# Expert stage of a four-layer fp32 model: three groups gathered at once, three passes written out, one looped

## The chip, the cores and the metric

The kernel runs on one core of a Trainium2 chip. The metric is the device time of one launch in microseconds (us), the median of several runs.

## The reference

Two blocks of two layers each, over 256 tokens of width 1024, all in fp32. Each layer has a mixer and then a hierarchical mixture of experts. This is the part that the change touches; layers 0 and 1 have 4 groups of 4 experts and also add a gated term, layers 2 and 3 have 4 groups of 8 experts.

```python
def hier_moe(h, wgc, bgc, wgf, bgf, w1, w3, w2):
    ...
    pg = jax.nn.softmax(jnp.dot(t, wgc, preferred_element_type=f32) + bgc.astype(f32), axis=-1)
    gw, gi = lax.top_k(pg, 1)
    fl = (jnp.dot(t, wgf, preferred_element_type=f32) + bgf.astype(f32)).reshape(T, N_GROUPS, EXPERTS_PER_GROUP)
    ...
    tv, ti = lax.top_k(jax.nn.softmax(fs, axis=-1), TOP_K_IN_GROUP)
    ...
    a = jnp.einsum('td,edf->tef', t, w1)
    c = jnp.einsum('td,edf->tef', t, w3)
    act = jax.nn.silu(a) * c * gates[:, :, None].astype(t.dtype)
    y = jnp.einsum('tef,efd->td', act, w2)

# first block, layers 0 and 1:
        y_ple = jax.nn.sigmoid(h @ ple_wg[i] + ple_bg[i]) * (p[i] @ ple_wp[i])
        h = layer_norm(DN_ALPHA * h + y_moe + y_ple, ln2_g[i], ln2_b[i])
```

Each token picks one group and two experts in it. A group has its own expert weights; a group that more than 128 tokens picked needs a second pass over the same weights.

## The kernel before

**The stream of weights.** All large weights come as units of 1 MB (128 x 2048 fp32). Four queues run in a fixed order over the same units: SyncE starts two DMAs of 512 KB into one of `RING` = 4 slots (`load`, L388 to L394) as soon as the unit four places earlier has been split; ScalarE copies the unit to a rounded high part (`split`, L1298 to L1304), for which one of `PARTS` = 3 buffers must be free, so the unit three places earlier used up; VectorE subtracts it for the low part (`split`, L1776 to L1781); TensorE multiplies high by high, low by high and high by low (`three`, L622 to L625), always 128 x 512 wide here. So one unit is 12 matmuls where one block of 128 tokens is used and 24 where both are.

**One expert** is three units: two for the two input projections (`up(e, 0)`, `up(e, 1)`, 24 matmuls) and one for the output projection (`down(e)`, 12 matmuls). Between them ScalarE makes the silu (L1386), VectorE multiplies it with the other half and the gate (L2040), TensorE transposes the product (L783), ScalarE and VectorE make its high and low parts (L1394, L2049), and `down(e)` follows. The order on TensorE is `up(e, 0)`, transposes of expert e - 1, `up(e, 1)`, `down(e - 1)`, so that this chain is covered by the next expert's matmuls.

**One pass** handles up to 128 tokens of one group: E experts (4 in layers 0 and 1, 8 in layers 2 and 3). All passes are iterations of one hardware loop on each engine (`Fori(0, passes)`, L761 on TensorE, L1373, L2025), 4 of them with these inputs (the program allows 5). The tokens of a pass are gathered by matmuls with a 0/1 matrix `SP` (32 matmuls of 128 x 128 in two parts, `gather`, L735 and L736, and four for the gates, L741, L742). The first part of the next gather and the gates are put around the transposes of the last expert, ahead of `down(E - 1)`; the second part comes at the head of the next iteration. The result of pass p - 1 is scattered in pass p, after `up(0, 1)`, by 8 matmuls of 128 x 512 (`scatter`, L750), in the first pass with zeros. After the loop comes the last scatter, and VectorE adds the four banks to X (L2070).

**Ahead of the loop** (`experts`, L676, L1321, L1886): transposes of the tokens (L640), logits (48 matmuls with the tokens stationary and 20 or 36 columns moving), some 55 small VectorE instructions that wait for each other and choose the group, the two experts, the gates (up to L1944), the slot `KEY` of each token (up to L1956) and the table of passes (up to L1968); then all engines read the number of passes, TensorE clears six banks (L727), VectorE builds `SP` (L2006), and the first gather follows. In layers 0 and 1 four units of 24 matmuls (the gated term) lie between; GpSimd multiplies and adds that term (L588 to L592). In layer 1 the 16 transposes of the second block's memory input lie there as well.

## Time and profile before

| | |
|---|---|
| median of 3 runs | 1811.83 us (1811.3 to 1812.22) |
| the profiled execution | 1805.22 us, of which the profile spans 1803.4 us |
| mean granted TensorE clock | 0.936 |
| TensorE matmul busy | 90% of the span |
| VectorE, ScalarE, GpSimd busy | 73%, 58%, 7% |
| DMA | 402.36 MB, mean 223 GB/s |

The profile lists for each group of instructions the line, the engine, the operation with the tiles that it writes and reads, a count, the busy time and the mean duration of one. In a timeline each row has the start and the duration in us, and in brackets how long the engine had stood idle and what ended that. Matmuls overlap, so a row's duration is longer than the distance to the next; distances between starts are used here. The busy share of TensorE is modelled in the same way and is an upper bound.

### The profile page before, as it was taken

To read this page: it belongs to the slowest core of one execution; us is meant where nothing else is said; L and a number is where in the kernel's file an instruction comes from. 1 tells how busy PE (TensorE), PEld (TensorE's weight loads), DVE (VectorE), ACT (ScalarE), POOL (GpSimd) and SP (SyncE) were. 2 spreads that over 40 slices of the span, in tenths; PEclk is the share of its full clock that TensorE was granted. 3 is DMA by queue.
4 is the path that set the end of the run, shared out by engine and by line. 5 is a ranking of instruction groups with operands and counts; after the bars stand their busy time and mean duration, and the time that the engine had idled before them with its cause. 6 is when DMAs were issued, how large, how long until landed. Compare 5 with 4: busy or idle time off the path is not lost.

```text
span 1803.4 us, 22655 instructions
## 1 busy us (share of the span) xinstructions
PE 1616.8 (90%) x7718; PEld 1332.0 (74%) x7718; DVE 1314.4 (73%) x1614; ACT 1038.5 (58%) x1151; POOL 129.1 (7%) x195
## 2 busy tenths in 40 slices
PE   5997999969879799979978999999798869999997
PEld 4876777858767678858866887878687657878786
DVE  6757588876667688874656878888775458888886
ACT  3543477744434577636424777777475326777774
POOL 3001400030022300000010000000000200000000
PEclk9997899989998899999977999999899959999998
DMA  8324388865334588844424989999542309999995
GB/s 309 125 92 154 116 296 304 301 226 171 128 96 155 179 306 306 307 168 141 152 86 158 364 294 342 335 306 369 162 144 71 97 24 302 312 362 306 361 313 186
DMA packets 282833, 402.36 MB, mean 223 GB/s; under 512 B 15962, under 2 KB 220538, under 8 KB 282512
## 3 DMA queue, kind: packets, MB, share of 16 engines
q1 hardware_dynamic: 273632, 381.99, 62.1%
q0 software_dynamic: 9136, 19.54, 3.7%
q8 instruction: 36, 0.59, 0.1%
q14 instruction: 29, 0.24, 0.0%
HBM read 400.43 MB, written 1.05 MB: 223 GB/s over the span
## 4 chain that ended last, share of the span: by engine, by line
PE 55%; DVE 19%; ACT 9%; DMA 9%; issue 7%; SPq 1%; DVEq 0%; ACTq 0%
PE bank L623 15%; PE bank L625 14%; PE bank L624 14%; DVE w_lo_at L1779 8%; ACT w_hi_at L1303 6%; DMA raw_at<-in_moe_w_up_dram 4%; PE bank L640 2%; DMA raw_at<-in_moe_w_down_dram 2%; DMA raw_at<-in_w_in_dram 1%; PE bank L735 1%; PE bank L736 1%; DMA raw_at<-in_moe_w_dram 1%; PE bank L830 1%; DVE x_at L1834 1%; DVE sel_at L2006 1%
## 5 line engine op out<-in xcount | busy, mean ns | idle before, releaser
L1779 DVE TENSOR_TENSOR w_lo_at<-raw_at,w_hi_at 128x2048 fp32r<-128x2048 f32 (+1 forms) x365 | 830.7, 2283 | 179.1 <-ACT w_hi_at L1303 168.6
L1303 ACT ACTIVATE w_hi_at<-raw_at 128x2048 fp32r<-128x2048 f32 (+1 forms) x365 | 694.1, 1907 | 102.9 <-PE bank L625 48.6
L623 PE MATMUL bank<-w_hi_at,xs_hi_at 128*128 128x512 f32 x768 | 315.2, 410 | 9.1 <-DVE w_lo_at L1779 5.5
L625 PE MATMUL bank<-w_hi_at,xs_lo_at 128*128 128x512 f32 x768 | 304.1, 396 | 0.0
L624 PE MATMUL bank<-w_lo_at,xs_hi_at 128*128 128x512 f32 x768 | 302.8, 394 | 0.0
L623 PE MATMUL bank<-w_hi_at,t_hi_at 128*128 128x512 f32 (+3 forms) x560 | 223.8, 400 | 17.2 <-DVE t_lo_at L1786 5.2
L624 PE MATMUL bank<-w_lo_at,t_hi_at 128*128 128x512 f32 (+3 forms) x560 | 216.9, 387 | 0.0
L625 PE MATMUL bank<-w_hi_at,t_lo_at 128*128 128x512 f32 (+3 forms) x560 | 216.8, 387 | 0.0
L623 PEld LDWEIGHTS bank<-w_hi_at,xs_hi_at 128*128 128x128 f32 x768 | 146.4, 191 | 50.0 <-DVE w_lo_at L1779 13.1
L625 PEld LDWEIGHTS bank<-w_hi_at,xs_lo_at 128*128 128x128 f32 x768 | 145.9, 190 | 33.3
L624 PEld LDWEIGHTS bank<-w_lo_at,xs_hi_at 128*128 128x128 f32 x768 | 146.4, 191 | 27.9
L623 PE MATMUL bank<-w_hi_at,act_hi_at 128*128 128x512 f32 x384 | 154.4, 402 | 9.6 <-DVE act_lo_at L2049 9.4
L624 PE MATMUL bank<-w_lo_at,act_hi_at 128*128 128x512 f32 x384 | 152.4, 397 | 0.0
L625 PE MATMUL bank<-w_hi_at,act_lo_at 128*128 128x512 f32 x384 | 152.0, 396 | 0.0
L623 PEld LDWEIGHTS bank<-w_hi_at,t_hi_at 128*128 128x128 f32 x560 | 109.0, 195 | 42.6 <-issue 17.7
L625 PEld LDWEIGHTS bank<-w_hi_at,t_lo_at 128*128 128x128 f32 x560 | 108.6, 194 | 20.6
L624 PEld LDWEIGHTS bank<-w_lo_at,t_hi_at 128*128 128x128 f32 x560 | 109.1, 195 | 18.9 <-issue 0.5
L1394 ACT ACTIVATE act_hi_at<-bank 128x256 fp32r<-128x256 f32 x96 | 36.8, 383 | 112.4 <-PE bank L783 73.3
L623 PEld LDWEIGHTS bank<-w_hi_at,act_hi_at 128*128 128x128 f32 x384 | 72.5, 189 | 30.5 <-issue 13.3
L625 PEld LDWEIGHTS bank<-w_hi_at,act_lo_at 128*128 128x128 f32 x384 | 72.9, 190 | 17.4
L624 PEld LDWEIGHTS bank<-w_lo_at,act_hi_at 128*128 128x128 f32 x384 | 72.8, 190 | 15.5
L1386 ACT ACTIVATE silu_at<-bank 128x256 f32<-128x256 f32 x96 | 36.8, 384 | 78.2 <-PE bank L625 77.6
(485 smaller groups left out, 2089.3 us busy)
## 6 DMA issues: line engine op xcount, KB each, us to landing
raw_at<-in_moe_w_dram SPq DMA_DIRECT2D x192, 512.0 KB, 4.9
raw_at<-in_moe_w_gate_dram SPq DMA_DIRECT2D x128, 512.0 KB, 5.0
raw_at<-in_moe_w_up_dram SPq DMA_DIRECT2D x128, 512.0 KB, 6.0
raw_at<-in_moe_w_down_dram SPq DMA_DIRECT2D x128, 512.0 KB, 5.4
raw_at<-in_w_in_dram SPq DMA_DIRECT2D x40, 512.0 KB, 5.2
raw_at<-in_a_w_in_dram SPq DMA_DIRECT2D x20, 512.0 KB, 4.7
raw_at<-in_w_out_dram SPq DMA_DIRECT2D x16, 512.0 KB, 4.3
raw_at<-in_ple_wg_dram SPq DMA_DIRECT2D x16, 512.0 KB, 4.9
```

What stands on the lines that cost most here:

```text
L623: pe.matmul(out, ah, bh, start=start, stop=False, skip_group_check=loose)
L624: pe.matmul(out, ah, bl, start=False, stop=False, skip_group_check=loose)
L625: return pe.matmul(out, al, bh, start=False, stop=stop, skip_group_check=loose)
L640: ins = pe.transpose(BK[b][:, c * T + tb * P:c * T + tb * P + P], block_, IDENT)
L735: pe.matmul(o, HH[:, tb, a:a + P], SP[:, tb, :], start=tb == 0, stop=False)
L736: ins = pe.matmul(o, HL[:, tb, a:a + P], SP[:, tb, :], start=False, stop=tb == 1)
L830: ins = pe.matmul(out, mat[:, kb, cols], rhs(kb), start=kb == 0, stop=kb == 1)
L1303: act.activation(WH[:, s.part(), 0:width], RAW[:, s.slot(), 0:width], ACT.Copy).then_inc(hi_done, 1)
L1386: act.activation(SIL[:, :], BK[6 + e % 2][:, 0:256], ACT.Silu).then_inc(*m.silu.tick(e))
L1394: act.activation(AH[:, :, :], BK[6 + e % 2][:, 0:256].rearrange("p (c t) -> p c t", t=P), ACT.Copy).then_inc(*m.ah.tick(e))
L1779: dve.tensor_tensor(WL[:, s.part(), 0:width], RAW[:, s.slot(), 0:width], WH[:, s.part(), 0:width].bitcast(F32), ALU.subtract).then_inc(spl ...
L1834: go(dve.scalar_tensor_tensor(x_, x_, by[:, tb:tb + 1], ROW[:, slot, 0:width], op1, op2))
```

## The change

- **Passes.** The first three passes (groups 0, 1, 2) are written out and chained: `up(0, 0)` of pass p + 1 follows `down(E - 2)` of pass p, with the transposes of the last expert behind it and `down(E - 1)` behind `up(0, 1)`. The loads follow the same order and the first three groups' need no table. Only the passes from the fourth on (one, with these inputs) run in a hardware loop, with their own gather; the loop body begins with the first half of the gather, the last expert's transposes and `down(E - 1)` of the pass before.
- **Gather.** The three groups' tokens are gathered at once: 8 chunks of four matmuls of 128 x 384 (`SP3`), each chunk in a bank of its own, copied out as `XH3` and `XL3`. They go ahead of the computing of the gates, and the matmuls that gather the gates go behind the first expert's `up`.
- **Logits.** The router's weights are stationary (high and low part side by side, `RWHL`), the 256 tokens move: 16 matmuls, one ScalarE copy with the bias, four fp32 matmuls that turn the result (`turn_logits`).
- The clearing of banks is gone (the first scatter starts them), and so is the first pass's scatter of zeros. The routing's slot arithmetic is shorter. The scatter comes behind `up(1, 0)`.
- GpSimd's work on the gated term moves to VectorE (`gated`), in two halves.
- The memory input's transposes move from layer 1's prelude into its third pass, one group per expert.
- Two splits of expert units are put ahead of the last `add_and_measure` steps in layers 2 and 3.

```diff
             def experts(L):
...
-                for tb in range(TB):
-                    for c in range(DC):
-                        t_ = slice(tb * P, tb * P + P)
-                        ins = three(BK[6][:, tb * 64:tb * 64 + NR[L]], TH[:, c, t_], TL[:, c, t_],
-                                    RWH[:, c, 0:NR[L]], RWL[:, c, 0:NR[L]], c == 0, c == DC - 1)
+                for c in range(DC):
+                    pe.matmul(BK[6][0:2 * N, 0:T], RWHL[:, c, 0:2 * N], TH[:, c, :], start=c == 0, stop=False,
+                              skip_group_check=True)
+                    ins = pe.matmul(BK[6][0:N, 0:T], RWHL[:, c, 0:N], TL[:, c, :], start=False, stop=c == DC - 1,
+                                    skip_group_check=True)
...
-                for b in range(6):
-                    ins = pe.matmul(BK[b][:, :], ZR[:, :], HH[:, 0, 0:512], start=True, stop=True)
-                ins.then_inc(*small_ready.tick(("cleared", L)))
...
+                pe.wait_ge(*dve_ready.at(("sel", L)))
+                for c, b in enumerate(GATHER):
+                    claim(b)
+                    o, a = BK[b][:, 0:3 * P], slice(c * P, c * P + P)
+                    for tb in range(TB):
+                        pe.matmul(o, HH[:, tb, a], SP3[:, tb, :], start=tb == 0, stop=False)
+                        ins = pe.matmul(o, HL[:, tb, a], SP3[:, tb, :], start=False, stop=tb == 1)
+                    ins.then_inc(*gathered.tick((L, c)))
+                    owner[b] = xl_ready.at((L, c))
...
+                for p in range(3):
+                    cols = slice(p * P, p * P + P)
+                    for e in range(E):
...
+                        before = (p, e - 1) if e else (p - 1, E - 1)
+                        if (p, e) == (0, 0):
+                            pe.wait_ge(*xl_ready.at((L, 3)))
+                        claim(6 + e % 2)
+                        up(e, 0, (XH3, XL3), cols)
+                        if e == 1 and p:
+                            claim(2, 3)
+                            scatter(p - 1, p == 1)
+                        if (p, e) == (0, 0):
+                            pe.wait_ge(*xl_ready.at((L, 7)))
+                        else:
+                            turn_glu(*before)
+                        up(e, 1, (XH3, XL3), cols)
+                        if (p, e) == (0, 0):
+                            key_row()
+                            gates()
+                        else:
+                            claim(4, 5)
+                            down(*before, memory)
...
+                with pe.Fori(3, passes) as p:
...
+                    pe.wait_ge(*m.sel.at(p - 3))
+                    gather(0).then_inc(*m.gather_a.tick())
+                    turn_glu(p - 1, E - 1, gather_gates)
+                    down(p - 1, E - 1)
+                    gather(1).then_inc(*m.gather_b.tick())
+                    pe.wait_ge(*m.xl_a.at(p - 3))
+                    up(0, 0, (XH, XL))
+                    pe.wait_ge(*m.xl_b.at(p - 3))
+                    up(0, 1, (XH, XL))
+                    for e in range(1, E):
+                        up(e, 0, (XH, XL))
+                        if e == 1:
+                            scatter(p - 1)
+                        turn_glu(p, e - 1)
+                        up(e, 1, (XH, XL))
+                        down(p, e - 1)
```

VectorE's order in a written-out step and at the head of the loop body:

```diff
+                            glu(*before, gate3(*before))
+                            split()
+                            if e == 1:
+                                slots(ch)
+                                low_y(p - 1)
+                            split()
+                            low(*before)
...
+                with dve.Fori(3, passes) as p:
...
+                    glu(p - 1, E - 1, GS[:, E - 1:E])
+                    split()
+                    low_x(0, m.xh_a, m.xl_a, p)
+                    split()
+                    dve.wait_ge(*m.at.at(p - 1, E - 1))
+                    dve.tensor_copy(GS[:, :], BK[7][:, 256:264]).then_inc(*m.gs.tick())
+                    low(p - 1, E - 1)
+                    low_x(1, m.xh_b, m.xl_b, p)
+                    slots(lc)
+                    low_y(p - 1)
```

## Rows read from the trace of the kernel before

**Rows 1.** Windows: stretch, length, busy time by engine, granted clock, DMA share, GB/s.
```profile
934.00:966.00 32.00, 19.85 (x85) 18.60 (x84) 14.45 (x63) 5.64 (x7) 0.00 (x0) 0.50 0.10 34
1122.00:1198.00 76.00, 75.23 (x353) 61.38 (x353) 64.30 (x51) 55.02 (x46) 0.00 (x0) 1.00 0.99 333
```
**Rows 2.** Timeline of ScalarE, layer 2, third pass: the same step, one expert apart.
```profile
1159.53 1.91 ACT L1303 ACTIVATE w_hi_at<-raw_at 128x2048 fp32r<-128x2048 f32 x1
...
1168.07 1.91 ACT L1303 ACTIVATE w_hi_at<-raw_at 128x2048 fp32r<-128x2048 f32 x1
```
**Rows 3.** Timeline of TensorE, layer 2, between second and third pass, and at the end.
```profile
1111.58 0.44 PE L623 MATMUL bank<-w_hi_at,act_hi_at 128*128 128x512 f32 x1
...
1114.40 0.22 PE L735 MATMUL bank<-sel_at,tok_hi_at 128*128 128x128 f32 x1
...
1117.65 0.47 PE L623 MATMUL bank<-w_hi_at,act_hi_at 128*128 128x512 f32 x1 [0.71 <-DVE act_lo_at L2049]
...
1127.97 0.39 PE L750 MATMUL bank<-ys_hi_at,sel_t_at 128*128 128x512 f32 x1
...
1129.79 0.39 PE L623 MATMUL bank<-w_hi_at,xs_hi_at 128*128 128x512 f32 x1
...
1263.15 0.40 PE L623 MATMUL bank<-w_hi_at,act_hi_at 128*128 128x512 f32 x1
```
**Rows 4.** The page, costliest groups: the two splits.
```profile
L1779 DVE TENSOR_TENSOR w_lo_at<-raw_at,w_hi_at 128x2048 fp32r<-128x2048 f32 (+1 forms) x365 | 830.7, 2283 | 179.1 <-ACT w_hi_at L1303 168.6
L1303 ACT ACTIVATE w_hi_at<-raw_at 128x2048 fp32r<-128x2048 f32 (+1 forms) x365 | 694.1, 1907 | 102.9 <-PE bank L625 48.6
```
**Rows 5.** Timeline of ScalarE, layer 2, second pass: three units apart.
```profile
1095.48 1.92 ACT L1303 ACTIVATE w_hi_at<-raw_at 128x2048 fp32r<-128x2048 f32 x1 [0.70 <-DMA raw_at<-in_moe_w_up_dram]
...
1104.20 1.92 ACT L1303 ACTIVATE w_hi_at<-raw_at 128x2048 fp32r<-128x2048 f32 x1 [0.70 <-DMA raw_at<-in_moe_w_up_dram]
```
**Rows 6.** Timeline of VectorE: the adds that end each layer's expert stage.
```profile
384.50 2.48 DVE L2070 TENSOR_TENSOR x_at<-x_at,bank 128x512 f32<-128x512 f32 x4 [2.23 <-PE bank L750]
...
774.21 2.48 DVE L2070 TENSOR_TENSOR x_at<-x_at,bank 128x512 f32<-128x512 f32 x4 [2.27 <-PE bank L750]
...
1276.70 2.48 DVE L2070 TENSOR_TENSOR x_at<-x_at,bank 128x512 f32<-128x512 f32 x4 [2.77 <-PE bank L750]
...
1796.37 2.48 DVE L2070 TENSOR_TENSOR x_at<-x_at,bank 128x512 f32<-128x512 f32 x4 [3.15 <-PE bank L750]
```
**Rows 7.** Timeline of VectorE, layer 2, end of the second pass.
```profile
1113.60 0.47 DVE L2040 SCALAR_TENSOR_TENSOR glu_at<-silu_at,gate_sel_at,bank 128x256 f32<-128x256 f32 x1
```
**Rows 8.** Timeline of layer 2 ahead of its loop, TensorE and VectorE.
```profile
931.83 0.26 PE L623 MATMUL bank<-rw_hi_at,t_hi_at 128*128 128x36 f32 x1 [1.50 <-DVE t_lo_at L1786]
...
940.27 0.30 DVE L1908 TENSOR_TENSOR logits_at<-bank,route_b_at 128x36 f32<-128x36 f32 x2 [5.18 <-PE bank L625]
...
949.47 0.16 DVE L1956 TENSOR_TENSOR key_at<-v_at,v_at 128x2 f32<-128x2 f32 x1
...
955.43 0.48 DVE L2006 TENSOR_SCALAR sel_at<-consts_at,key_at 128x128 fp32r<-128x128 f32 x2 [0.84 <-DVE key_row_at L1998]
...
966.37 0.73 PE L623 MATMUL bank<-w_hi_at,xs_hi_at 128*128 128x512 f32 x1
```
**Rows 9.** Timeline of layer 0 ahead of its loop, TensorE, GpSimd and VectorE.
```profile
200.69 0.39 PE L625 MATMUL bank<-w_hi_at,t_lo_at 128*128 128x512 f32 x1
...
204.03 2.40 POOL L588 TENSOR_TENSOR y_at<-y_at,sg_at 128x1024 f32<-128x1024 f32 x1
...
204.20 3.53 DVE L2006 TENSOR_SCALAR sel_at<-consts_at,key_at 128x128 fp32r<-128x128 f32 x2 [1.10 <-issue]
...
214.10 0.73 PE L623 MATMUL bank<-w_hi_at,xs_hi_at 128*128 128x512 f32 x1
```
**Rows 10.** Timeline of TensorE: first expert matmul of layers 1 and 3.
```profile
600.22 0.45 PE L623 MATMUL bank<-w_hi_at,xs_hi_at 128*128 128x512 f32 x1
...
1486.55 0.73 PE L623 MATMUL bank<-w_hi_at,xs_hi_at 128*128 128x512 f32 x1
```

More of the change, by code:

```diff
@@ L477, in _ @@
+                s.unit, s.turns = unit, sp.snap(start + (passes - 3) * turns)
+                last = sp.value_load(TAB[0:1, bass.ds(passes, 1)], min_val=0, max_val=3)
+                down(last, E - 1)
             for tb in range(TB):
@@ L819, in experts @@
+                s.unit, s.turns = unit, pe.snap(start + (passes - 3) * turns)
+                turn_glu(passes - 1, E - 1)
+                down(passes - 1, E - 1)
+                scatter(passes - 1).then_inc(*small_ready.tick(("moe", L)))
                 for b in range(8):
@@ new lines, in high_y, with step @@
+                def high_y(back):
+                    act.wait_ge(unit_used, s.count(back))
+                    for half in range(2):
+                        act.activation(YH[:, half * 512:half * 512 + 512], BK[4 + half][:, :], ACT.Copy)\
+                           .then_inc(*m.yh.tick())
+                def step(p, e):
+                    before = (p, e - 1) if e else (p - 1, E - 1)
+                    silu(*before, -2)
+                    split()
+                    if e == 1:
+                        high_y(-2)
+                    split()
+                    high(*before)
@@ L1404, in _ @@
+                        split()
+                s.unit, s.turns = unit, act.snap(start + (passes - 3) * turns)
+                silu(passes - 1, E - 1, -2)
+                split()
+                high(passes - 1, E - 1)
+                high_y(-1)
             root("ln0", 2)
@@ L1993, in experts @@
[L1993 to L2001 removed]
+                    dve.wait_ge(*rows_in.at(("ple", L)))
+                    add_rows(0)
```

767 lines of the change are left out of this document (418 added, 349 removed).

## The prediction

> **What bounds the kernel now.** I read the four expert stages, since the change touches nothing else of weight. The windows view first: a pass of layer 2 takes 76 us at a granted clock of 1.00 and 333 GB/s, while the 32 us ahead of its loop move 34 GB/s at a clock of 0.50, the lower of the two levels [rows 1]. So inside a pass several resources are nearly full, and ahead of the loop none is. What paces the inside is seen on ScalarE: the same split comes back after 8.54 us, one expert later [rows 2]. TensorE needs 36 matmuls for that; eight matmuls of the same width take 1129.79 - 1127.97 = 1.82 us [rows 3], 0.227 each, so 8.2 us plus two transposes, about 8.4. The splits alone are 3 x 2.28 = 6.8 us on VectorE and 3 x 1.91 = 5.7 on ScalarE [rows 4], under that. DMA is the near rival: where each split waits for its landing, three units come in 1104.20 - 1095.48 = 8.72 us [rows 5]. The reader is to see that 8.54 times 8 is 68.3, and with the scatter's 1.82 it is 70.1, while the pass takes 76: some 6 us lie at its boundary. There down(6) starts at 1111.58, the first part of a gather at 1114.40, down(7) only at 1117.65, behind 20 small matmuls, the transposes and 0.71 us of idling, then come 16 more gather matmuls, and the next scatter at 1127.97 [rows 3].
>
> **The sum's form.** A stage ends with the adds to X. From the effective start S of the experts (the first expert matmul, moved by what delays that first expert) I count N experts at 8.54 (N = 32 or 16), three scatters at 1.82 (5.5; the fourth is in the tail), two chained boundaries, one loop entry, and a tail. Tail: down(6) starts at 1263.15 [rows 3] and the adds at 1276.70 [rows 6], 13.55, of which two `down` units (24 x 0.227 = 5.45) are already in N x 8.54, leaving 8.1. The change leaves it: the gather matmuls in it go (they filled the wait for the last expert's low part), but the wait stays since VectorE's split lies in the same place, and the low parts of Y now wait for both halves. Bounds for the tail -1.5 to +1.
>
> *Chained boundary.* Gathers, gates, clock dips and the idle gap go. A new wait comes: the scatter moves behind `up(1, 0)` and needs the low part of Y. VectorE ends the glu 2.5 us after the last `up` unit ended (1111.58 to 1113.60 + 0.47 [rows 3, 7]); then a split (2.28), two slot instructions (about 0.5) and two low parts (about 1.3), so ready at 6.6, while `up(1, 0)`, behind the 12 matmuls of down, is over at 5.5. TensorE waits about 1.2 us; queued behind are the transposes and `up(1, 1)`, and ScalarE's high part waits for them. Nothing is late enough to add. Two per layer: 2.4 (bounds 0 to 4).
>
> *Loop entry.* This is dearer than the old boundary. In the body VectorE does glu, a split, a low part of x, a second split and the gate copy before the last expert's low part, and ScalarE's high part waits for the gate copy. From the end of the last `up` unit: glu over at 3.5 (ScalarE has a table load ahead of the silu), first split 6.4, low x 7.0, second split 9.4, copy, high, low 10.5; down then runs to 13.3, gather to 15.1. In the chained order three units would be done by 11; here it is one. Counting on to `up(1, 1)`, it starts at 26.1 against 16.3, so 9.8 is added. TensorE stands idle for about 5 us of that; if the clock falls to the lower level as in the 0.50 window [rows 1], one to four us come on top. I take 12 (bounds 6, the present boundary, and 15).
>
> *The prelude of layers 2 and 3.* Before: logits from 931.83, first routing instruction 940.27, KEY 949.47, the first selection 955.43, first expert matmul 966.37 [rows 8]. The 45 small VectorE instructions from 940.27 to KEY take 9.2, so 0.20 each. After: the logits are 16 matmuls in place of 48, 2 to 4 us instead of 8.4, but VectorE is not there earlier: ScalarE does a split and the token copy (2 x 1.9) from 931.0, VectorE then 2 x 2.28, so 939.4. Gain 0.9, and one split that stood behind the table is already done. 12 small instructions, the ranks (TensorE, until about 943.0), 7 more: KEY at 944.4; six compares of about 0.25: selection ready at 945.9. TensorE gathers 32 x 128x384: at 0.75 of 0.227 it is 5.4 us, at the lower clock 10.2, over between 951.4 and 956.2. VectorE computes gates and table meanwhile (about 33 instructions, 6.8) until 952.8, then four low parts of 384 columns (0.55, estimated between the 128x512 and 128x256 ones): 955.1. Behind the first expert come key row and gates, 1.8 us. S = 956.9 (bounds 954 to 960), where the first matmul was at 966.4. The six clears and a scatter of zeros are gone as well. The hoisted splits of these layers fall into VectorE's wait for the mixer's last strips; if that cover fails they cost up to 2.3 each.
>
> *The prelude of layers 0 and 1.* Before, the gated term's last unit ended at 200.69 + 0.2; six clears and the gathers followed, the first expert matmul at 214.10; VectorE's two selection compares took 3.53 us there against 0.48, while GpSimd multiplied [rows 9, 8]. After: the fourth unit waits for VectorE, which has routing, gates and table first and then the split; counting the same small instructions at 0.20 I place that split's end at 189.5, so the unit runs to 194.9. VectorE then has two splits (4.6), half of the gated term (2.6, four 128x512 at about 0.65) and the bias adds (2 x 1.3), so banks 2 and 3 come free for the last two gather chunks at 202.6, and the first expert matmul is at 204.9. Behind it VectorE is late again: a split, the other half of the gated term, the selection for the loop and a split lie ahead of the first glu, and the first transposes wait until 217.0. That makes S = 208.9; I add 1.5 for a lowered clock: 210.4 (bounds 206 to 214). Layer 1, with the same steps and 6 us of memory norm on VectorE, gives S = 591.4 (first matmul before: 600.22 [rows 10]; bounds 587 to 597). Its moved transposes cost 1.8 in the third pass.
>
> **The sum.** E = 8: 273.3 + 5.5 + 2.4 + 12 + 8.1 = 301.3. Layer 2: 956.9 + 301.3 = 1258.2 against 1276.7, gain 18.5. Layer 3 is layer 2 moved by 1486.55 - 966.37 [rows 10, 8]: 1477.1 + 301.3 = 1778.4 against 1796.4, 18.0. E = 4: 136.6 + 28.0 = 164.6. Layer 0: 375.0 against 384.5, 9.5. Layer 1: 591.4 + 164.6 + 1.8 = 757.8 against 774.2, 16.4 [rows 6]. Together 62.4. The profiled execution took 1805.22 and its span 1803.4; it becomes 1742.8. The median of the three runs, 1811.83, is 6.6 above the profiled one; I keep that offset: 1811.8 - 62.4 = 1749.4.
>
> Against two rules. The loop's back edges, of which three per layer go, show no price: from 1117.65 to 1127.97 [rows 3], with one among it, are 10.3 us, of which 36 matmuls at 0.227 are 8.2 and 16 gathers at about 0.11 are 1.8; 0.4 is left for everything else. The Trainium skill (Runtime: NRT & Kernel Launch, Instruction fetch mechanics) says that a taken branch outside the prefetched pages stalls its engine for a fetch; by that the written-out passes would gain a little more than the sum has, by the row nothing. And DMA, which in the late stretch brings three units in 8.72 us: the Trainium skill (DMA: Bandwidth & Descriptors, Specifications) gives about 358 GB/s from HBM for one core, so 8.79 us for an expert's 3.146 MB; eight would be 70.3, and the chained pass has 71.3 by my sum, so that would cost next to nothing; rows and rule differ by 0.07.
>
> **The rivals.**
> (A) *DMA becomes the bound.* Now each boundary gives the ring of four slots 6 us to fill up; chained passes give 3. For: the late stretch at 8.72 per expert [rows 5]. Against: eight at 8.72 are 69.8, under 71.3. With fewer pauses to catch up in, suppose 9.2: 73.6 - 71.3 = 2.3 in each of six chained passes of layers 2 and 3, 14 us, and about 3 in each of their looped ones (73.6 against 70.1), 7; passes of 4 (36.8 against 37.2) lose nothing. 1749 + 21 = 1770.
> (B) *The loop entry is cheap and the clock holds.* 6 instead of 12 in four layers, and the starts at their early bounds (3, 3, 3, 4): 24 + 13 gives 1712; half of it 1731.
> (C) *Chaining doesn't close the boundary:* the queues' fixed order makes TensorE wait as long as now (the wait for Y's low part, the late glu). Then eight boundaries cost 6 instead of 1.2: 38 less gain: 1788.
> (D) *Slower.* The written-out passes make a steady step longer: one engine's straight code, three passes of it in place of a loop body, stalls each expert by some time. 72 experts lie there; from 62.4 / 72 = 0.87 us a step the change loses. For: VectorE's step is 6.8 + 0.47 + 0.42 plus waits of some 8.0 of 8.54 us, so that any stall of 0.5 there is on the path. Against: the order of a step is unchanged, and the mixers' straight code runs matmuls at the same 0.227. At 1.3 us a step: 1811.8 - 62 + 94 = 1843.
> (E) *It doesn't do what it says*, e.g. the preludes start no earlier since VectorE's queue has everything ahead: S gains (9.5, 9.4, 3.7, 8.8) gone: 31 less: 1780.
>
> **Chances.** Forecast 0.55 (its own range 1736 to 1763); A 0.13; B 0.14; C 0.07; D 0.04; E 0.07. The predicted time is 1749. The range takes in A and half of B: 1725 to 1774; what is left out is C, D, E and the far half of B, about 0.2. A measurement of this kernel can tell 0.2% (3.6 us) from no change. Faster 0.94, within 0.2% 0.02, slower 0.04.
>
> **What would show it.** The first expert matmul of layers 2 and 3 about 23 us after the first of the logits (34.5 before), in layer 0 about 10 us after the gated term's last unit (13 before); an `up(0, 0)` spacing of 71.3 us (E = 8) and 37.2 (E = 4) in the chained passes, with a TensorE gap of about 1.2 ahead of the scatter; one pass per layer with a gap of about 5 us ahead of `down(E - 1)` and perhaps a clock dip; ScalarE's splits waiting for TensorE, not DMA. DMA waits at most splits would speak for A; steps over 8.7 with neither DMA nor the scatter as cause for D. The prediction is wrong if the loop entry or the layer 0 prelude is off by more than 5 us, since I placed those instructions.

## The result and the profile after

The changed kernel takes 1755.1 us (median of 4 runs, 1754.0 to 1756.6), the kernel before on the same chip 1812.0: a ratio of 0.968, 95% interval 0.966 to 0.970. It is faster by 57 us. The prediction was 1749, with a range from 1725 to 1774.

The profiled execution took 1754.0, its span is 1751.9. The page of the changed kernel: busy time and share of the span by engine, and the two splits.

```profile
PE 1542.5 (88%) x7230; PEld 1263.8 (72%) x7230; DVE 1302.8 (74%) x1580; ACT 999.2 (57%) x1123; POOL 95.7 (5%) x187
...
L1875 DVE TENSOR_TENSOR w_lo_at<-raw_at,w_hi_at 128x2048 fp32r<-128x2048 f32 (+1 forms) x365 | 832.5, 2283 | 158.5 <-ACT w_hi_at L1356 148.0
L1356 ACT ACTIVATE w_hi_at<-raw_at 128x2048 fp32r<-128x2048 f32 (+1 forms) x365 | 695.0, 1907 | 117.7 <-PE bank L623 65.6
```

The splits are what they were [rows 4]. TensorE has 488 matmuls fewer, and its busy time fell by 74 us, more than the span did. The adds to X in the timeline of VectorE end the four expert stages, as in [rows 6]:

```profile
372.61 2.48 DVE L2232 TENSOR_TENSOR x_at<-x_at,bank 128x512 f32<-128x512 f32 x4 [3.66 <-PE bank L755]
...
758.24 1.88 DVE L2232 TENSOR_TENSOR x_at<-x_at,bank 128x512 f32<-128x512 f32 x3 [3.71 <-PE bank L755]
...
1241.65 2.48 DVE L2232 TENSOR_TENSOR x_at<-x_at,bank 128x512 f32<-128x512 f32 x4 [3.27 <-PE bank L755]
...
1744.90 2.48 DVE L2232 TENSOR_TENSOR x_at<-x_at,bank 128x512 f32<-128x512 f32 x4 [3.52 <-PE bank L755]
```

To compare stage by stage I take the length from the adds to X that end the mixer to these ones. The same instruction, an `up(e, 0)`'s first matmul, gives the parts. "Start" is the start that the prediction calls S (worked back from the third expert, 14.2 us before it), counted from the mixer's adds; "tail" runs from the start of `down(E - 2)` to the adds, less 5.45 us for two `down` units, as in the prediction. The loop entry is counted over three steps of 8.54.

| us, forecast / measured | start | the two chained scatter steps, over 8.54 | loop entry with its scatter | tail | stage | gain on before |
|---|---|---|---|---|---|---|
| layer 0 | 68.1 / 64.5 | 3.0 / 3.2, 2.9 | 13.8 / 14.2 | 8.1 / 10.4 | 232.7 / 231.7 | 9.5 / 10.5 |
| layer 1 | 70.4 / 70.6 | 3.0 / 3.1, 6.2 | 13.8 / 17.8 | 8.1 / 9.6 | 236.8 / 249.0 | 16.4 / 4.2 |
| layer 2 | 42.3 / 40.7 | 3.0 / 3.6, 3.2 | 13.8 / 13.8 | 8.1 / 8.6 | 343.6 / 342.9 | 18.5 / 19.2 |
| layer 3 | 42.8 / 40.9 | 3.0 / 3.6, 2.9 | 13.8 / 13.3 | 8.1 / 8.8 | 344.1 / 343.5 | 18.0 / 18.5 |

Nearly all other steps are 8.53 us, but in layer 1's third pass they are 11.2. The stages gain 52.5 where 62.4 were forecast, and layer 1 alone is short by 12.2. Outside the stages 1.3 came in ahead of layer 0, 0.2 was lost in two mixers and 2.1 in layer 3's: 51.5, the difference of the two spans.

Where does the gain lie? Count from the mixer's adds to the third expert's first matmul, here in layer 2, kernel before and changed kernel:

```profile
985.25 0.50 PE L623 MATMUL bank<-w_hi_at,xs_hi_at 128*128 128x512 f32 x1 [0.30 <-DVE w_lo_at L1779]
```

```profile
953.69 0.40 PE L621 MATMUL bank<-w_hi_at,xs_hi_at 128*128 128x512 f32 x1
```

With adds at 914.64 and 898.76 that is 70.6 us before and 54.9 after. The four layers gain 11.1, 15.7, 15.7 and 15.6 us there, 58 together, so the preludes and the scatter of zeros hold the whole gain. The three pass boundaries of a layer, with their scatters, took 22.2, 23.4 and 22.2 us in layers 0, 2 and 3 and take 20.4, 20.6 and 19.8; in layer 1 they went from 22.4 to 27.1. Two chained boundaries are cheaper than the old ones, and the loop entry takes most of that back. Layer 1's third pass and longer tails then eat some 5 of the 58.

The windows view answers [rows 1]. Its columns are those of [rows 1]: layer 2's prelude, eight experts across the boundary into its third pass (from expert 4 to expert 4), and `down(3)` in layer 0's loop entry.

```profile
908.00:938.00 30.00, 17.97 (x83) 16.83 (x84) 21.52 (x70) 11.84 (x19) 0.56 (x1) 0.66 0.17 58
1042.90:1114.30 71.40, 70.30 (x314) 56.88 (x313) 62.53 (x45) 52.30 (x42) 0.00 (x0) 1.00 1.03 354
...
319.00:324.40 5.40, 5.38 (x13) 4.23 (x14) 0.00 (x0) 0.00 (x0) 0.00 (x0) 0.50 0.63 201
```

Eight experts across that boundary take 71.4 us where a pass took 76, and move 354 GB/s instead of 333. Across the boundary before it they take 72.2.

The third pass of layer 1 is where the missing time lies. The timeline of the three engines, changed kernel, around one expert of that pass:

```profile
654.20 0.60 PE L800 MATMUL bank<-consts_at,mem_at 128*128 128x128 f32 x4
...
659.61 0.50 PE L621 MATMUL bank<-w_hi_at,xs_hi_at 128*128 128x512 f32 x1 [2.02 <-DVE w_lo_at L1875]
...
654.83 0.60 ACT L1455 ACTIVATE xs_hi_at<-bank 128x512 fp32r<-128x512 f32 x1 [2.83 <-PE bank L800]
655.33 1.91 ACT L1356 ACTIVATE w_hi_at<-raw_at 128x2048 fp32r<-128x2048 f32 x1
...
655.47 0.69 DVE L2185 TENSOR_TENSOR xs_lo_at<-bank,xs_hi_at 128x512 fp32r<-128x512 f32 x1 [1.89 <-ACT xs_hi_at L1455]
657.26 2.29 DVE L1875 TENSOR_TENSOR w_lo_at<-raw_at,w_hi_at 128x2048 fp32r<-128x2048 f32 x1 [1.11 <-ACT w_hi_at L1356]
```

Read it backwards. TensorE stands at 659.61 for VectorE's split. That split started at 657.26, because ScalarE's half of it ran from 655.33. ScalarE had been free since 652.0 (the rows of ScalarE and VectorE follow TensorE's above), and the next instruction in its queue was the copy of the memory transposes, which TensorE only does at 654.20. So an instruction that nobody needs for 100 us held up one that TensorE needs at once.

And the loop entry, layer 0 (TensorE, then VectorE):

```profile
313.40 0.25 PE L849 MATMUL bank<-gate_lo_at,sel_at 128*128 128x8 f32 x1
319.02 0.79 PE L621 MATMUL bank<-w_hi_at,act_hi_at 128*128 128x512 f32 x1 [5.36 <-DVE act_lo_at L2135]
...
311.58 0.48 DVE L2130 SCALAR_TENSOR_TENSOR glu_at<-silu_at,gate_sel_at,bank 128x256 f32<-128x256 f32 x1 [1.16 <-issue]
311.97 2.29 DVE L1875 TENSOR_TENSOR w_lo_at<-raw_at,w_hi_at 128x2048 fp32r<-128x2048 f32 x1
314.18 0.68 DVE L2152 TENSOR_TENSOR xs_lo_at<-bank,xs_hi_at 128x512 fp32r<-128x512 f32 x1
315.54 2.29 DVE L1875 TENSOR_TENSOR w_lo_at<-raw_at,w_hi_at 128x2048 fp32r<-128x2048 f32 x1 [0.68 <-ACT w_hi_at L1356]
317.75 0.16 DVE L2201 COPY gate_sel_at<-bank 128x8 f32<-128x8 f32 x1
318.45 0.42 DVE L2135 TENSOR_TENSOR act_lo_at<-bank,act_hi_at 128x256 fp32r<-128x256 f32 x1 [0.55 <-ACT act_hi_at L1423]
```

This is the gap of about 5 us that the prediction placed there, behind the very instructions it named. The matmuls of `down(3)` behind it come 0.43 us apart where the full clock has 0.23.

### The profile page after: what moved, and what is told of

It reads as the page before. It is cut to its first block, busy times and chain, and to the rows that moved or that the text cites. A ratio compares the mean times of both kernels' runs of the same rounds, so it can differ in the third digit from the quotient of the medians.

```text
span 1751.9 us, 20547 instructions
## 1 busy us (share of the span) xinstructions
PE 1542.5 (88%) x7230; PEld 1263.8 (72%) x7230; DVE 1302.8 (74%) x1580; ACT 999.2 (57%) x1123; POOL 95.7 (5%) x187
## 3 DMA queue, kind: packets, MB, share of 16 engines
q1 hardware_dynamic: 273632, 381.99, 64.5%
## 4 chain that ended last, share of the span: by engine, by line
PE 65%; DVE 17%; ACT 8%; DMA 5%; issue 4%; SPq 0%; DVEq 0%; ACTq 0%
PE bank L621 17%; PE bank L623 16%; PE bank L622 16%; DVE w_lo_at L1875 7%; ACT w_hi_at L1356 5%; DMA raw_at<-in_moe_w_up_dram 2%; PE bank L755 2%; PE bank L638 2%; DMA raw_at<-in_moe_w_dram 1%; PE bank L774 1%; PE bank L883 1%; DVE x_at L1930 1%; DMA raw_at<-in_moe_w_down_dram 1%; DVE stats_at L1943 1%; DVE ys_lo_at L2147 1%
## 5 line engine op out<-in xcount | busy, mean ns | idle before, releaser
L621 PE MATMUL bank<-w_hi_at,xs_hi_at 128*128 128x512 f32 x800 | 325.3, 407 | 14.7 <-DVE w_lo_at L1875 10.8
L623 PE MATMUL bank<-w_hi_at,xs_lo_at 128*128 128x512 f32 x800 | 316.5, 396 | 0.0
L622 PE MATMUL bank<-w_lo_at,xs_hi_at 128*128 128x512 f32 x800 | 314.5, 393 | 0.0
L621 PE MATMUL bank<-w_hi_at,t_hi_at 128*128 128x512 f32 (+3 forms) x528 | 209.8, 397 | 12.2 <-DVE t_lo_at L1882 5.2
L622 PE MATMUL bank<-w_lo_at,t_hi_at 128*128 128x512 f32 (+3 forms) x528 | 203.2, 385 | 0.0
L623 PE MATMUL bank<-w_hi_at,t_lo_at 128*128 128x512 f32 (+3 forms) x528 | 203.0, 385 | 0.0
L623 PEld LDWEIGHTS bank<-w_hi_at,xs_lo_at 128*128 128x128 f32 x800 | 151.6, 189 | 34.3
L621 PEld LDWEIGHTS bank<-w_hi_at,t_hi_at 128*128 128x128 f32 x528 | 102.1, 193 | 36.5 <-issue 14.8
L623 PEld LDWEIGHTS bank<-w_hi_at,t_lo_at 128*128 128x128 f32 x528 | 102.1, 193 | 18.8
L622 PEld LDWEIGHTS bank<-w_lo_at,t_hi_at 128*128 128x128 f32 x528 | 102.5, 194 | 17.3 <-issue 0.5
```

Source lines behind the costliest of these rows:

```text
L621: pe.matmul(out, ah, bh, start=start, stop=False, skip_group_check=loose)
L622: pe.matmul(out, ah, bl, start=False, stop=False, skip_group_check=loose)
L623: return pe.matmul(out, al, bh, start=False, stop=stop, skip_group_check=loose)
```

## The experiments

Each started from the changed kernel (1755.1 us), and its ratio stands against the kernel before on its own chip. That kernel took 1812.0 us beside the changed kernel and 1809.4 to 1810.2 beside these, so a difference of some 2 us between two times means nothing. Four theories were to be told apart: what held layer 1, what the loop entry's 12 us are, where the preludes' gain is from, and what paces the steady step.

**The memory copies behind the split (e1).** ScalarE's edit; VectorE's copy moves in the same way.

```diff
                             step(p, e)
+                            split()
                             if L == DEPTH - 1 and p == 2:
...
-                            split()
```

> Edit on the changed kernel (1755.1 us): in layer 1's third pass ScalarE's and VectorE's copies of the memory transposes stand behind the step's last split instead of ahead of it. Theory (queue order): in the changed kernel ScalarE's next split starts at 655.33, behind the copy that waits for TensorE's transposes, where it could start at 652.0, and TensorE waits for VectorE's split until 659.61, 2.2 us after the last matmul. With the copies behind the split the four steps of that pass fall from 11.2 to 11.3 (14.7 with the scatter) to 8.53 plus the transposes' 0.35, so about 8.9 (12 with the scatter); layer 1's stage ends 9 to 11 us earlier and nothing else moves: 1745 us. Rival (the cost is TensorE's own: the transposes, their banks, or DMA): the steps stay at 11.2 and the time at 1755.

Measured: 1744.4 us (ratio 0.963, 0.960 to 0.966). The pass's steps are 8.95, 12.41 and 8.98. VectorE now takes the split first, and nothing stands ahead of TensorE's next unit. (The two views: VectorE, TensorE.)

```profile
654.63 2.29 DVE L1875 TENSOR_TENSOR w_lo_at<-raw_at,w_hi_at 128x2048 fp32r<-128x2048 f32 x1 [0.61 <-ACT w_hi_at L1356]
656.84 0.68 DVE L2186 TENSOR_TENSOR xs_lo_at<-bank,xs_hi_at 128x512 fp32r<-128x512 f32 x1
...
658.19 0.40 PE L621 MATMUL bank<-w_hi_at,xs_hi_at 128*128 128x512 f32 x1
```

From the pass's first expert to the loop's first it is 54.9 us in place of 64.1; the same stretch of layer 0 takes 52.0 in the changed kernel. So of the 12.1 us of extra time 9.2 were the order of the queues. The transposes' own 4 x 0.4 are what the prediction had priced at 1.8, and some 1.3 are left open. The rival, TensorE or DMA, is out as the main cause.

**The low part first in the loop's head (e2).** VectorE's order; ScalarE's high part moves ahead of x's likewise.

```diff
                     split()
-                    low_x(0, m.xh_a, m.xl_a, p)
-                    split()
                     dve.wait_ge(*m.at.at(p - 1, E - 1))
                     dve.tensor_copy(GS[:, :], BK[7][:, 256:264]).then_inc(*m.gs.tick())
                     low(p - 1, E - 1)
+                    low_x(0, m.xh_a, m.xl_a, p)
+                    split()
```

> Edit on the changed kernel (1755.1 us): in the loop's head VectorE does the gate copy and the last expert's low part ahead of x's first low part and the second split, and ScalarE its high part ahead of x's. Theory (queue order, then clock): TensorE's idle gap ahead of down(E - 1), 313.5 to 319.0 in layer 0, shrinks to 1 to 2 us; the clock does not fall to 0.50 there, so that down's 12 matmuls take 2.8 instead of 5.3 us. About 4 + 2.5 in each of four layers: 26, so 1729 us. Rival 1 (clock falls for another reason): only the idle goes, 4 x 4 = 16, 1739. Rival 2 (the loop entry's price is register loads, branches or the new gather, not this order): under 4 us in all, 1752 or more.

Measured: 1738.3 us (ratio 0.961, 0.956 to 0.965), 17 less. The loop entries with their scatter are 8.2, 14.4, 9.6 and 9.6 us, from 14.2, 17.8, 13.8 and 13.3. The gap shrank as forecast, in layer 0 (first row) and layer 2 alike. The clock came out both ways. Below are the first matmul of `down(E - 1)` in layer 0 and in layer 2, then a window over each of these units:

```profile
317.95 0.50 PE L621 MATMUL bank<-w_hi_at,act_hi_at 128*128 128x512 f32 x1 [1.79 <-DVE act_lo_at L2135]
...
1145.58 0.50 PE L621 MATMUL bank<-w_hi_at,act_hi_at 128*128 128x512 f32 x1 [1.59 <-DVE act_lo_at L2135]
...
317.90:320.80 2.90, 2.85 (x12) 2.37 (x13) 1.79 (x2) 1.74 (x1) 0.00 (x0) 1.00 0.99 373
1145.50:1150.00 4.50, 4.42 (x12) 3.53 (x13) 2.89 (x2) 1.67 (x1) 0.00 (x0) 0.62 0.86 314
```

With the clock held, layer 0 gained 6.0 us; with it lost for a part, layers 2 and 3 gained 4.3 and 3.7. So the order of the queue is the cause of the gap, and the theory was 9 us too high in that it had the clock stay up everywhere. The time, 1738, is the 1739 of rival 1, in which only the idle time goes: the clock fell in layer 2 behind a gap of only 1.6 us. Rival 2 (register loads, branches) is out as the main cause.

**The slots first in the scatter's step (e3).**

```diff
-                            split()
                             if e == 1:
                                 slots(ch)
                                 low_y(p - 1)
                             split()
+                            split()
```

> Edit on the changed kernel (1755.1 us): in the chained passes' second step VectorE does the slot instructions and the low parts of Y ahead of its first split. Theory: TensorE's 1.2 to 1.5 us ahead of each chained scatter goes (the scatter starts with the end of up(1, 0)), and the split moved behind is ready 6.9 us after the last up unit, just ahead of its use: steps with a chained scatter 10.4 instead of 11.4 to 12.1, eight of them, 9 to 12 us: 1745. Rival: TensorE then waits for that split instead, the step stays at 11.4 or more: 1755.

Measured: 1746.4 us (ratio 0.965, 0.962 to 0.968), 9 less. The scatter row of the changed kernel in layer 0, and the same with this edit, behind the last matmul of `up(1, 0)`:

```profile
249.34 0.47 PE L755 MATMUL bank<-ys_hi_at,sel_t_at 128*128 128x512 f32 x1 [1.12 <-DVE ys_lo_at L2147]
```

```profile
248.45 0.39 PE L623 MATMUL bank<-w_hi_at,xs_lo_at 128*128 128x512 f32 x1
248.68 0.39 PE L755 MATMUL bank<-ys_hi_at,sel_t_at 128*128 128x512 f32 x1
```

Seven of the eight scatter steps are now 1.77 to 1.82 over 8.54, the bare scatter (the eighth lies in layer 1's third pass, held by the memory copies). The prediction's 1.2 us for the new wait is what went, 1.1 to 1.8 each.

**All three (e4).**

> The edits of the three kernels before it together. Theory: they lie in different steps, so they add: 10 + 26 + 10 = 46 less than the changed kernel, 1709 us. Rival (DMA becomes the bound once the pauses are gone, 8.72 us for three units as in the late stretch of the kernel before, 72 experts in chained passes, 0.19 each, and no pause left to catch up in): 14 us are given back, 1723, and steps of 8.7 and more stand in the chained passes with splits waiting for landings.

Measured: 1715.2 us (ratio 0.947, 0.944 to 0.950), 40 less than the changed kernel, where the three alone gave 10.7, 16.8 and 8.7, so 36: they add, to within what the runs differ by (those of e2 alone lie between 1735 and 1745). Eight experts of layer 2, across the boundary into its third pass:

```profile
1017.30:1087.50 70.20, 70.20 (x313) 56.74 (x312) 62.02 (x44) 52.56 (x42) 0.00 (x0) 1.00 1.04 357
```

TensorE has no idle time left there, 8 x 8.53 + 1.82 = 70.1; the eight before them take 70.0. The DMA rival took nothing in these two; in layer 3 the steps that are not scatters exceed 8.54 by 1.3 us in sum, where the changed kernel has 0.5.

**The selection behind the gates (e5).** The six compares stand behind the gates' instructions, as one part of the change undone.

```diff
-                for g in range(3):
-                    for tb in range(TB):
-                        go(dve.tensor_scalar(SP3[:, tb, g * P:g * P + P], IOTA, 128.0 * g, KEY[:, tb:tb + 1], ALU.add, ALU.is_equal))
-                done(("sel", L))
...
                 done(("gates", L))
+                for g in range(3):
...
+                done(("sel", L))
```

> One part of the change undone (from 1755.1 us): the six selection compares, and with them the gathers, wait until VectorE has the gates. Theory: in layers 2 and 3 the selection is what the gather waits for, and the gates' instructions between take 5.7 us (929.2 to 934.6 and a little), so the gather and the first expert matmul come 5.5 to 7 us later in each: 1767 us. In layers 0 and 1 the gather starts 14 us after the selection is ready, so nothing moves there. Rival: VectorE's low parts of x, which start at 935.7 behind the table, set the first expert anyway, and only 2 us per layer are lost: 1759.

Measured: 1764.0 us (ratio 0.976, 0.973 to 0.978), 9 more. The gather of layer 2 starts 5.5 us later, but the first expert matmul only 4.5 us (3.8 in layer 3), counted from the mixer's adds. TensorE, the changed kernel and this one:

```profile
929.15 0.69 PE L727 MATMUL bank<-sel_at,tok_hi_at 128*128 128x384 f32 x1 [2.36 <-DVEq L1867]
...
937.77 0.49 PE L621 MATMUL bank<-w_hi_at,xs_hi_at 128*128 128x512 f32 x1
```

```profile
934.73 0.69 PE L727 MATMUL bank<-sel_at,tok_hi_at 128*128 128x384 f32 x1 [7.86 <-DVEq L1867]
...
942.31 0.39 PE L621 MATMUL bank<-w_hi_at,xs_hi_at 128*128 128x512 f32 x1
```

From the gather's first matmul to the expert's it is 8.6 us in one and 7.6 in the other. So putting it ahead of the gates is worth 8 us for both layers, less than the 11 to 14 expected and more than the rival's 4. Layers 0 and 1 did not move, as expected.

**Two passes written out instead of three (e6),** in layers 0, 2 and 3.

```diff
+        W = [2, 3, 2, 2]
-                for p in range(3):
+                for p in range(W[L]):
-                with pe.Fori(3, passes) as p:
+                with pe.Fori(W[L], passes) as p:
```

> From the changed kernel (1755.1 us): in layers 0, 2 and 3 only two passes are written out and the loop runs from the third on, two rounds in place of one; layer 1 is as it was. Theory (the gain of chaining is the difference of the two boundaries): from the last expert's start to the third expert of the next pass the chained boundary takes 28.5 to 29.2 us and the loop's 39.9, 39.5 and 38.8, so three boundaries more in the loop cost 11.4 + 10.3 + 9.9 = 32: 1787 us, with steps of 8.53 inside either. Rival (written-out code has a price of its own, such as fetching instructions, which the loop doesn't pay; or the loop's first round holds a cost that a second one doesn't repeat, such as its entry's register loads): under 20 us more, 1775 or less, and steps that are shorter in the looped passes than in the written-out ones.

Measured: 1782.7 us (ratio 0.985, 0.983 to 0.988), 27.6 more; the stages grew by 9.0, 12.5 and 13.6 in the profiled execution, the longest of its four. The passes of layer 2, one chained, two looped:

```profile
977.10:1049.00 71.90, 70.51 (x313) 56.65 (x312) 62.44 (x45) 52.54 (x42) 0.00 (x0) 1.00 1.02 351
1049.00:1131.90 82.90, 77.18 (x349) 62.97 (x348) 63.87 (x51) 52.29 (x44) 0.00 (x0) 0.94 0.88 302
1131.90:1214.80 82.90, 76.90 (x350) 62.39 (x350) 65.20 (x52) 53.39 (x45) 0.00 (x0) 0.96 0.88 305
```

Steps inside are 8.53 in either kind. The loop's first round and its second are both 82.9 us long, but the second has one step of 9.08 in it; from the last expert of one pass to the first of the next, the first round takes 23.8, 23.8 and 23.5 us (layers 2, 3, 0) and the second 23.2, 23.4 and 23.2. So at most 0.3 to 0.6 us is paid once on entering. Of the 11 us between 71.9 and 82.9, e2 has shown 4 to 6 to be the order in the loop's head; the rest, with the loop's own gathers in it, was not taken apart. These 11 us set the two kinds of this kernel against each other. Against the kernel before, with its 76 us, a chained pass saves 4 and a looped one costs 7 more. Written-out code shows no price of its own.

**Less work for TensorE (e7), and half the bytes besides (e8).**

```diff
-                            ins = three(BK[4 + half][:, :], AH[:, f, :], AL[:, f, :], WH[:, s.part(), a:a + 512],
...
+                            pe.matmul(BK[4 + half][:, :], AH[:, f, :], WH[:, s.part(), a:a + 512],
...
+                            ins = pe.matmul(BK[4 + half][:, :], AH[:, f, :], WL[:, s.part(), a:a + 512],
...
```

> What paces the steady step of 8.53 us? This kernel leaves out the third product of every down unit (the activations' low part times the weights' high part), so each expert has 32 matmuls in place of 36, 0.92 us less for TensorE; nothing else changes. If TensorE alone paces, the chained steps fall from 8.53 to about 7.65 (VectorE's three splits, glu and low part, 3 x 2.2 + 0.4 + 0.4 = 7.4, allow it). If DMA stands right behind (8.72 for three units in the late stretch of the kernel before), they stay between 8.4 and 8.7, with ScalarE's splits waiting for landings.

> As the kernel before it, and every expert unit loads only half of its columns (the rest of the buffer is what lay there), so half the bytes. If DMA was what held that kernel's steps, they fall to about 7.65 here; if VectorE or the order of the queues held them, they stay where they were. Routing may come out another way in the later layers, so only the steps inside passes are read.

Measured: 1754.1 and 1701.1 us, one execution each. Neither computes the reference's result in full: e7 leaves out a product, and e8 also multiplies what lay in the buffers, so only the steps are read. With the third product left out, the first steps behind a pause are 7.8 us and then they return to 8.4 to 9.1 (from the fifth expert of layer 2's second pass on 8.74, 8.48, 8.39, 9.06, 8.57: 8.65 in the mean), a few to 9.6 and more, and ScalarE waits for landings. Eight experts across a boundary take 70.5 to 73.1 us in layers 2 and 3, where the changed kernel has 71.1 to 72.2, and the whole time stays where it was. With half the bytes nearly every steady step is 7.82 to 7.89. ScalarE with all the bytes, then eight experts of layer 2 in either (354 GB/s was the changed kernel's):

```profile
985.11 1.92 ACT L1358 ACTIVATE w_hi_at<-raw_at 128x2048 fp32r<-128x2048 f32 x1 [0.65 <-DMA raw_at<-in_moe_w_up_dram]
```

```profile
1041.30:1111.80 70.50, 66.00 (x280) 49.88 (x280) 62.22 (x45) 51.77 (x43) 0.00 (x0) 1.00 1.02 351
```

```profile
1019.40:1086.00 66.60, 65.08 (x282) 50.33 (x281) 61.96 (x45) 50.50 (x43) 0.00 (x0) 1.00 0.62 190
```

So TensorE paces the changed kernel, and DMA stands 0.1 us behind it: rival (A) was close, and held off only by what the ring catches up with in the scatter and the boundaries.

**The logits as before (e9).**

```diff
-                for c in range(DC):
-                    pe.matmul(BK[6][0:2 * N, 0:T], RWHL[:, c, 0:2 * N], TH[:, c, :], start=c == 0, stop=False,
...
+                for tb in range(TB):
+                    for c in range(DC):
+                        t_ = slice(tb * P, tb * P + P)
+                        ins = three(BK[6][:, tb * 64:tb * 64 + N], TH[:, c, t_], TL[:, c, t_],
+                                    RWHL[:, c, 0:N], RWHL[:, c, N:2 * N], c == 0, c == DC - 1)
```

> One part of the change undone (from 1755.1 us): the logits are computed as in the kernel before, 48 small matmuls with the tokens stationary, the bias added by VectorE, no turning back. Theory (the prediction's): in layers 2 and 3 VectorE is busy until 923.2 with the token's low part and a split, and the 48 matmuls, 8.4 us in the kernel before, would end at about 924.4, so the selection comes about 1.5 us later (less if the clock rises in them): 3 for both. In layers 0 and 1 TensorE's 4 to 6 us more lie ahead of the gated term's units, which are followed by the gather; up to 4 each if TensorE's order sets the start, nothing if VectorE's splits do. 1755 + 3 to 11: 1758 to 1766. Rival (the stationary weights are what brings the preludes forward): 5 us or more in each of layers 2 and 3.

Measured: 1770.4 us (ratio 0.980, 0.975 to 0.985), 15 more. Layers 2 and 3 lose 1.1 and 0.2 us, near the 0.9 that the prediction had, and the rival is out. Layers 0 and 1 lose 7.9 and 7.5, twice what was expected. Two windows, from the first logits matmul to the first gather matmul in layer 0, changed kernel and this one:

```profile
165.70:192.70 27.00, 26.36 (x130) 21.69 (x131) 20.05 (x63) 14.04 (x13) 0.00 (x0) 1.00 0.37 117
```

```profile
167.10:200.70 33.60, 33.46 (x154) 28.72 (x155) 20.14 (x64) 13.56 (x12) 0.00 (x0) 0.85 0.29 94
```

TensorE is busy all through both, so the 24 matmuls more and a granted clock of 0.85 push the gather back by all of 6.6 us. The form of the logits is worth 15 of the change's 57 us, nearly all of it in the two layers whose prelude TensorE fills. With e5's 8 us that is 23 of the 58 gained ahead of the third experts. The first pass's scatter of zeros, at 1.8 us a layer by [rows 3], would be 7 more. What the dropped clearing of banks, the gated term's move to VectorE and the two splits put ahead of the last `add_and_measure` steps give or cost, no run takes apart.

**TensorE kept busy in the prelude (e10), and the low parts of x ahead of the gates (e11).** Both have the three edits in them, and belong beside e4.

```diff
+                def keep(n):
+                    for _ in range(n if L >= DEPTH else 0):
+                        pe.matmul(BK[5][:, :], TH[:, 0, 0:P], TH[:, 0:2, :].rearrange("p c t -> p (c t)"), start=True, stop=True)
...
                     turn_logits()
+                    keep(18)
                     ranks()
+                    keep(10)
```

> From the kernel with the three edits (1715.2 us): in layers 2 and 3 TensorE fills its waits ahead of the gather with 4 + 18 + 10 matmuls of 512 columns whose product nobody reads. The 32 gather matmuls of layer 2 took 8.4 us there, most of them at the lower clock; at the full one they are 5.4. Theory: the clock stays at 1.00 through the prelude and the gather ends 3 us earlier, but VectorE's low parts of x start only behind the table, so the first expert matmul comes at most 0.3 us earlier: 1715. Rival 1 (the clock falls whatever these matmuls do, and they delay the ranks): up to 2 us slower a layer, 1719. Rival 2 (TensorE's gather sets the start): 3 us a layer faster, 1709.

> As the kernel before it, and VectorE does the eight low parts of x directly behind the key diagonals, with the rest of the gates and the table behind them. Theory: with the gather at the full clock over at about 5.4 us after its start and the low parts following it, the first expert matmul of layers 2 and 3 comes 3 us earlier, and the gates, then ready 5 us after it, are not late for their matmuls behind the first expert's two units: 1715 - 6 = 1709. Rival (the clock isn't held): 0 to 1 us a layer, 1714.

Measured: 1717.8 (ratio 0.947, 0.942 to 0.952) and 1706.2 (ratio 0.941, 0.936 to 0.946). The gather of layer 2 in e4, e10 and e11:

```profile
905.70:914.40 8.70, 8.40 (x33) 8.09 (x33) 7.19 (x37) 3.69 (x9) 0.00 (x0) 0.68 0.01 3
```

```profile
903.90:909.50 5.60, 5.60 (x33) 5.52 (x32) 4.37 (x26) 2.79 (x8) 0.00 (x0) 1.00 0.00 0
...
912.52 0.79 PE L621 MATMUL bank<-w_hi_at,xs_hi_at 128*128 128x512 f32 x1 [2.78 <-DVE xs_lo_at L2124]
```

```profile
906.00:911.60 5.60, 5.60 (x33) 5.51 (x32) 4.75 (x21) 2.76 (x8) 0.00 (x0) 1.00 0.01 3
```

With the idle matmuls the clock was 1.00, and the gather fell by 3 us. Alone that gave nothing, since VectorE's low parts came next (the 2.78). With those moved forward too, the first expert matmul came 3.8 and 4.1 us earlier in layers 2 and 3. At 1706.2 us it is the fastest kernel here, 104 us under the kernel before. Its four runs lie at 1701 and at 1711, and its interval meets that of e4 (0.944 to 0.950), so its 9 us over e4 rest on the trace's 7.9 as much as on the medians.

## Why the prediction was right, and where not

*What bounds a pass* was right: a steady step stayed at 8.53 in every layer, 36 matmuls long, with DMA as the near rival (e7, e8). By the Trainium skill (DMA: Bandwidth & Descriptors, Specifications), whose limit is about 358 GB/s from HBM for one core, DMA would have needed an estimated 8.79 us an expert. The traces do not agree: they have steps of 8.53, and in the kernel held by DMA 8.65 (e7). In e10 the rate stayed at 365 GB/s over 100 us:

```profile
1510.00:1610.00 100.00, 100.00 (x444) 80.55 (x443) 88.37 (x63) 74.63 (x60) 0.00 (x0) 1.00 1.06 365
```

So the measurement decides, though for a pass with its scatter the two differ by little, as the prediction said. Written-out and looped steps are the same 8.53, and a round behind the loop's back edge is no dearer than the one that enters it (e6). So the rule of the Trainium skill (Runtime: NRT & Kernel Launch, Instruction fetch mechanics), that a taken branch outside the prefetched pages stalls its engine for a fetch, shows no price here. Whether this loop's body lies outside these pages no run shows.

*The chained boundary* was right in mechanism and size: a wait of 1.2 forecast behind the scatter's place, 1.1 to 1.8 measured, and gone when VectorE's order was changed (e3). The spacing of `up(0, 0)` from the second pass to the third is 71.8 in layer 2 (71.3 forecast) and 37.3 in layer 0 (37.2).

*The loop entry* was right: 13.8 with its scatter, measured 13.3 to 14.2 outside layer 1. One step of its working was wrong without harm: the glu was late not for a table load of ScalarE (the silu was over at 308.96) but because VectorE had a split and a copy of the gates, and then 1.16 us in which it waited for nothing that the profile shows; it ended 3.7 us after the last `up` unit, 3.5 forecast. And `down(E - 1)` ran at the lower clock, for which the forecast had allowed 1 to 4 us.

*The preludes* were right for layers 1 to 3 to within 2 us: 70.6, 40.7 and 40.9 from the mixer's adds, where 70.4, 42.3 and 42.8 were forecast; the selection was ready at 929.0, 13.1 us after the first logits matmul, where 14.1 were forecast, and the first expert matmul 21.8 us after it, where 23 were. Layer 0's came 3.6 us earlier than forecast. Its gather starts as the gated term's last unit ends, since TensorE and not VectorE is the late one (e9).

*The tail* was mis-sized by 0.5 to 2.3 us: 8.1 forecast, 8.6 to 10.4 measured. The prediction read it in layer 2 and said that the change leaves it. Measured in the same way the kernel before has 7.6 in layers 0 and 1, so the change lengthened it there by 2.9 and 2.0. The last scatter, kernel before and changed kernel, layer 0:

```profile
382.30:384.50 2.20, 2.08 (x8) 1.42 (x8) 0.00 (x0) 0.44 (x1) 0.00 (x0) 1.00 0.00 0
```

```profile
369.00:372.60 3.60, 3.56 (x8) 2.48 (x8) 0.00 (x0) 0.00 (x0) 0.00 (x0) 0.56 0.00 0
```

The same eight matmuls run at a granted clock of 1.00 in one and 0.56 in the other. Layer 0's last `down` unit has 0.62 too. The gather matmuls that used to fill TensorE's wait ahead of that unit are gone; that the clock fell for this reason is likely, and no run tests it.

*The moved memory transposes* are the step that failed. The prediction priced them at 1.8 us, about TensorE's own time for them, and gave nothing for what hangs on them: the copies of ScalarE and VectorE went into two queues ahead of a split that TensorE waits for. Against the same steps of layer 0 they cost 12.1 us: 3.3 in the scatter's step, 5.4 in two others and 3.5 at the loop entry. e1 gave back 9.2 of that. With 12.1 in place of 1.8 the sum would have had a gain of 52.1 us, where the spans differ by 51.5; the sum's other misses, in the starts, the tails and layer 3's mixer, nearly cancel.

*The total.* The sum gave 1742.8 for the profiled execution, and that took 1754.0: 11.2 too little (10.9 in the span). Layer 1 is 12.2 of it and the mixers 2.4; ahead of layer 0 and in the other three stages it came out 3.6 better. The median then lay 1.1 us above the profiled execution, where the prediction had carried over 6.6. So 1749 came within 6 us of 1755.1 partly by luck, because these two errors have opposite signs.

*Rivals.* (A) didn't come in this kernel, and is as close as it was said to be (e7). (B) didn't come: the loop entry was dear. (C) is out (a chained boundary costs 1.1 to 1.8 over its scatter, not 6), (D) is out (8.53 everywhere), (E) is out: every prelude is earlier.

*Layer 3's mixer*, 2.1 us slower, was in no term. Two windows each at the same place in it, of the kernel before and of the changed kernel:

```profile
1285.00:1291.20 6.20, 3.98 (x18) 3.64 (x19) 4.78 (x6) 3.67 (x5) 2.12 (x4) 0.67 0.57 74
1291.20:1293.50 2.30, 2.30 (x18) 2.30 (x17) 1.75 (x1) 0.52 (x1) 0.00 (x0) 1.00 0.93 351
```

```profile
1250.00:1256.50 6.50, 4.40 (x19) 4.00 (x20) 4.73 (x6) 3.97 (x5) 2.13 (x4) 0.50 0.54 84
1256.50:1260.00 3.50, 3.50 (x16) 3.50 (x16) 3.14 (x6) 0.22 (x1) 0.00 (x0) 0.55 0.74 279
```

The same matmuls run at the full clock in one and nearly all at the lower in the other, 18 in 2.3 us against 16 in 3.5: the clock came back later behind the stage's end. Why is open. In e9 and e11 that mixer took 158.1 and 158.3 us, near the 157.6 of the kernel before, in the changed kernel 159.8, and in e10 161.4.

## What to carry to other kernels

A step moved into another stage is priced on every queue that it touches: the transposes cost 1.6 us on TensorE, and their copies 9 more because they stood ahead of a split instead of behind it. In queues that run in order, put what somebody waits for next ahead of what nobody needs soon: three such swaps took 40 us from this kernel, without removing an instruction. Count a change's gain part by part, too: three passes are chained here, and the 57 us came in ahead of them. And when an engine is made faster, ask what comes next: the gather's 3 us were worth nothing until VectorE's order was changed too.

## What the runs showed of the hardware

The granted clock of TensorE costs time that a sum by full-speed rows misses. After a gap of 5.4 us in the loop's head the next 12 matmuls ran at 0.50, 5.3 us in place of 2.8; after gaps of 1.6 and 1.8 us it fell in layer 2 and not in layer 0. In the prelude of layers 2 and 3 a gather of 32 matmuls took 8.0 to 8.4 us with waits ahead of it (granted clock 0.68) and 5.5 with matmuls in those waits (1.00). DMA brought an expert's 3.146 MB in 8.65 us where it set the pace (364 GB/s), and in 8.53 (369 GB/s) over several experts in a row; over 100 us of e10 it moved 365 GB/s.
